# First-layer memory keys and values made inside the experts' loop in native fp32, and the down product put ahead of the up product from the seventh pair on

## What is computed

```python
# experts: the 256 tokens go to 4 of 32 experts each
u = xb @ w1[e] + b1[e]                      # w1[e]: 1024 x 2048 fp32, 8 MB
a = glu * sigmoid(SWIGLU_ALPHA * glu) * (lin + 1.0)
y = a @ w2[e] + b2[e]                       # w2[e]: 1024 x 1024 fp32, 4 MB

# first layer of the second model
h = x @ a_w_in                              # u, v, q_mem
mix = gmlp_mixer(u, v, ...)
kv = mem @ w_mem_kv[0]                      # mem: 256 x 1024, w_mem_kv[0]: 1024 x 512
k, v = split(kv)                            # keys and values of the memory, 4 heads of 64
s = softmax(q_mem . k * 64 ** -0.5); mem_out = s . v
x = layer_norm(ALPHA * x + concat(mix, mem_out) @ w_mix_out, ...)
```

## Time and profile before

| | |
|---|---|
| median of 3 runs | 1880.47 us |
| profiled execution, its own time | 1880.95 us |
| span of its instructions | 1879.2 us |
| PE busy | 1799.8 us (96%) |
| DVE, ACT busy | 773.2 us, 571.8 us |
| mean granted TensorE clock | 0.996 of full |
| DMA from slice 8 to slice 26 of 40 | 9 tenths or more, 426 to 432 GB/s in nearly all |
| chain that ended last | PE 79%, DMA 15%, DVE 3%, ACT 2% |

### The profile page before, as it was taken

The page is one execution under the profiler, slowest core; times in us unless marked ns, Lnnn a source line. Parts: engine busy times, 40 slices in busy tenths (PEclk is TensorE's granted clock), DMA queues, the critical chain, the costliest instruction groups (busy, mean ns, idle before and its releaser), DMA issues.

```text
span 1879.2 us, 24262 instructions
## 1 busy us (share of the span) xinstructions
PE 1799.8 (96%) x9774; PEld 1137.3 (61%) x9774; DVE 773.2 (41%) x1146; ACT 571.8 (30%) x913; POOL 16.5 (1%) x33
## 2 busy tenths in 40 slices
PE   7999999999999999989999999999999999999998
PEld 4799888733333333333333333337988888978886
DVE  3767655512112112121121111216676656676665
ACT  4444554410001100011000110005655545545552
POOL 0000001000000000000000000000000000000000
PEclk9999999999999999999999999999999999999999
DMA  9976755899999999999999999999356556336542
GB/s 353 328 249 226 246 198 189 316 427 426 431 431 430 431 430 430 429 431 429 430 431 429 432 430 430 431 430 341 134 180 199 182 202 202 121 105 205 197 170 100
DMA packets 155690, 592.39 MB, mean 315 GB/s; under 512 B 6735, under 2 KB 85775, under 8 KB 129120
## 3 DMA queue, kind: packets, MB, share of 16 engines
q1 hardware_dynamic: 153104, 582.90, 78.8%
q0 software_dynamic: 2512, 8.45, 1.4%
HBM read 590.26 MB, written 1.07 MB: 315 GB/s over the span
## 4 chain that ended last, share of the span: by engine, by line
PE 79%; DMA 15%; DVE 3%; ACT 2%; issue 1%; SPq 0%; DVEq 0%; ACTq 0%
PE psum L1781 18%; DMA expert_ring<-in_w_mlp_dram 13%; PE psum L426 9%; PE psum L1799 8%; PE psum L392 7%; PE psum L394 7%; PE psum L393 7%; PE psum L425 4%; PE psum L1765 4%; PE psum L410 2%; PE psum L1819 2%; PE psum L411 2%; PE psum L412 2%; DMA mixer_ring<-in_w_in_dram 1%; ACT expert_arena L1524 1%
## 5 line engine op out<-in xcount | busy, mean ns | idle before, releaser
L1781 PE MATMUL psum<-shared,expert_arena 128*64 128x512 f32 x1536 | 341.9, 597 | 18.9 <-DMA shared<-in_w_mlp_dram 18.9
L1627 DVE TENSOR_SCALAR expert_arena<-psum 128x512 f32<-128x512 f32 x32 | 22.1, 691 | 579.9 <-PE psum L1781 579.9
L1781 PEld LDWEIGHTS psum<-shared,expert_arena 128*64 128x64 f32 x1536 | 106.0, 137 | 238.6 <-issue 202.2
L426 PE MATMUL psum<-layer_x_parts,layer_w_hi 128*128 128x512 f32 x704 | 240.5, 396 | 0.4 <-DVE layer_x_parts L2131 0.4
L1530 ACT ACTIVATE expert_arena<-expert_arena 128x512 f32<-128x512 f32 x32 | 20.1, 629 | 559.4 <-DVE expert_arena L1627 559.4
L425 PE MATMUL psum<-layer_x_parts,layer_w_lo 128*128 128x256 f32 x616 | 171.8, 279 | 0.0
L353 DVE TENSOR_TENSOR mixer_w_lo<-mixer_ring,mixer_w_hi 128x1024 fp32r<-128x1024 f32 x96 | 116.3, 1222 | 88.7 <-ACT mixer_w_hi L348 88.1
L353 DVE TENSOR_TENSOR layer_w_lo<-slots_ahead,layer_w_hi 128x1024 fp32r<-128x1024 f32 x96 | 116.8, 1223 | 85.1 <-ACT layer_w_hi L348 85.1
L348 ACT CAST mixer_w_hi<-mixer_ring 128x1024 fp32r<-128x1024 f32 x96 | 100.0, 1048 | 151.6 <-PE psum L394 80.4
L426 PEld LDWEIGHTS psum<-layer_x_parts,layer_w_hi 128*128 128x128 f32 x704 | 125.8, 188 | 24.6 <-DVE layer_x_parts L2131 0.8
L392 PE MATMUL psum<-layer_w_hi,layer_x_parts 128*128 128x512 f32 (+1 forms) x368 | 134.2, 365 | 1.0 <-DVE layer_x_parts L2131 1.0
(11 more groups left out here) (324 smaller groups left out, 2630.2 us busy)
## 6 DMA issues: line engine op xcount, KB each, us to landing
shared<-in_w_mlp_dram SPq DMA_DIRECT2D x98, 2048.0 KB, 22.0
expert_ring<-in_w_mlp_dram SPq DMA_DIRECT2D x64, 2048.0 KB, 25.0
mixer_ring<-in_w_in_dram SPq DMA_DIRECT2D x38, 1024.0 KB, 7.0
slots_ahead<-in_w_mlp_dram SPq DMA_DIRECT2D x15, 2048.0 KB, 25.7
mixer_ring<-in_w_ada_dram SPq DMA_DIRECT2D x22, 1024.0 KB, 6.2
slots_ahead<-in_w_ffn_in_dram SPq DMA_DIRECT2D x22, 1024.0 KB, 5.0
memory_kv<-in_w_mlp_dram SPq DMA_DIRECT2D x15, 1024.0 KB, 24.7
kept<-in_w_mlp_dram SPq DMA_DIRECT2D x15, 1024.0 KB, 26.7
```

The lines of the kernel that those rows point to most:

```text
L426: last = self.nc.tensor.matmul(out, hi, both[:, k].rearrange("p h s -> p (h s)"), start=k == 0, stop=k == KC - 1)
L1781: last = nc.tensor.matmul(U[CAP * h:CAP * h + CAP, N * n:N * n + N], xg[:, k, j, :], expert_slot(M, k // 2)[:, at:at + N], start=False, st ...
```

## The change

1. In `on_sync`, `mem_2` and the final gain are issued ahead of the loop (after the last load for expert 1). The weights of the keys and values, `w_mem_kv_2[0]` (2 MB), are issued in the middle, behind the up pieces of expert 16, into `ahead`. The down pieces of expert 17 wait until the values are made (`memory_full`), since the memory's working tiles lie where they go.
2. PE runs `memory()` between pairs 7 and 8: 16 transposes in 4 groups through two banks that ACT empties, 16 products of 256 columns for the keys and 16 for the values, plain fp32. ACT copies the results out; PE waits for the last copy. After the loop ACT moves the values to `kv`.
3. From pair 6 on (TURN = 6) PE's order is `later_pairs_of`, with `down` ahead of `up`; ACT and DVE have loops to match (`turned`).
4. Layer 0 loses the jobs km0 and vm0 and their four units. Its scores now stand ahead of un1. The norm of v hangs on wsT0 instead of km0.

```diff
@@ experts @@
+    MIDDLE, TURN = PAIRS // 2, PAIRS // 2 - 2
...
@@ on_sync @@
                 second_odd(1, 1)
+                sp.dma_start(free(M["base"], 0, T, D), A["mem_2"][0].rearrange("(t p) d -> p t d", p=P)).then_inc(M["mem_here"], 16)
+                sp.dma_start(final_gain(M).unsqueeze(1), A["g_final"].rearrange("(o d) -> o d", o=1).partition_broadcast(P)).then_inc(M["fin_here"], 16)
...
+                    loads_of(1, MIDDLE)
+                    e = 2 * MIDDLE
+                    for k in range(UP):
+                        up_load_freed(e, e, k, True)
+                    sp.wait_ge(down_used, (e - 1) * DOWN + 1)
+                    sp.dma_start(M["ahead"][:, :], A["w_mem_kv_2"][0].rearrange("(p k) n -> p (k n)", k=KC)).then_inc(M["mem_here"], 16)
+                    for k in range(DOWN):
+                        down_load(e, e, k, 0, True)
+                    for k in range(UP):
+                        up_load_freed(e + 1, e + 1, k, True)
+                    sp.wait_ge(memory_full, VALUES)
+                    for k in range(DOWN):
+                        down_load(e + 1, e + 1, k, 1, True)
+                    loads_of(MIDDLE + 1, PAIRS - 1)
...
@@ on_scalar @@
+            def memory_rows_out():
+                for n in range(4):
+                    act.wait_ge(memory_full, n + 1)
+                    nc.scalar.copy(memT[:, 2 * n:2 * n + 2, :], bank[BG if n % 2 else BY].rearrange("p (k s) -> p k s", k=2)).then_inc(memory_out, 1)
+                act.wait_ge(memory_full, KEYS)
+                nc.scalar.copy(memory_keys(M), bank[BY].rearrange("p (a s) -> p a s", a=2)).then_inc(memory_out, 1)
+                act.wait_ge(memory_full, VALUES)
+                nc.scalar.copy(values_aside[:, :], bank[BG]).then_inc(memory_out, 1)
...
@@ on_vector @@
+                def turned(p):
+                    e = p * 2 + 1
+                    i = i0 + e
+                    gatedT_out(i - 1, 0)
+                    gate(r, e)
+                    dve.wait_ge(gathered, (r * PAIRS + p + 1) * 2)
+                    choose(r, p + 1)
+                    dve.wait_ge(down_used, (i - 1) * DOWN + 1)
+                    choose_own(e + 1, 0)
+                    y_out(i - 1)
+                    activate(i)
...
@@ on_tensor @@
+                    if ahead is not None and k == KC // 2:
+                        gather(ahead, 0)
...
+            def later_pairs_of(r, begin, end):
+                with pe.Fori(begin, end) as p:
+                    i = r * E + p * 2 + 1
+                    emptied(i - 1)
+                    down(i - 1, 0, r * PAIRS + p)
+                    up(i, r * PAIRS + p, 1, r * PAIRS + p + 1)
+                    scatter(i - 1, 0)
+                    gather(r * PAIRS + p + 1, 1)
+                    transposes(i)
+                    emptied(i)
+                    down(i, 1, r * (PAIRS - 1) + p)
+                    up(i + 1, r * PAIRS + p + 1, 0)
+                    scatter(i, 1)
+                    transposes(i + 1)
+
+            def memory():
+                pe.wait_ge(M["mem_here"], 16)
+                pe.wait_ge(down_used, 2 * MIDDLE * DOWN)
+                pe.wait_ge(xg_ready, 2 * MIDDLE + 2)
+                for n in range(4):
+                    if n >= 2:
+                        pe.wait_ge(memory_out, n - 1)
...
+                pe.wait_ge(M["mem_here"], 32)
+                pe.wait_ge(memory_out, 4)
+                for a in range(2):
+                    for k in range(KC):
+                        last = nc.tensor.matmul(bank[BY][:, N_MEM * a:N_MEM * a + N_MEM], w_mem[:, k, P * a:P * a + P], memT[:, k, :], start=k == 0, stop=k == KC - 1)
+                last.then_inc(memory_full, 1)
+                for t in range(T):
+                    for k in range(KC):
+                        last = nc.tensor.matmul(bank[BG][:, W_MEM * t:W_MEM * t + W_MEM], memT[:, k, P * t:P * t + P], w_mem[:, k, W_MEM:2 * W_MEM], start=k == 0, stop=k == KC - 1)
+                last.then_inc(memory_full, 1)
+                pe.wait_ge(memory_out, VALUES)
...
-            pairs_of(0, 0, middle)
+            pairs_of(0, 0, TURN)
+            later_pairs_of(0, TURN, MIDDLE)
+            memory()
...
@@ layer, i == 0 @@
         jobs.pair("vn1", "act", jobs.rows(w_in, W_MIX + N, W_MIX - N))
-        jobs.add("km0", "act", jobs.wide(w_kv[0], 0))
         for n in range(3):
             jobs.add(f"wsT{n}", "dve")
         jobs.add("bsT", "dve")
         jobs.pair("un0", "act", jobs.rows(w_in, 0))
         jobs.add("qm", "act", jobs.wide(w_in, 2 * W_MIX))
-        jobs.pair("un1", "act", jobs.rows(w_in, N, W_MIX - N))
         scores(0)
         scores(1)
+        jobs.pair("un1", "act", jobs.rows(w_in, N, W_MIX - N))
         for n in range(3):
             jobs.add(f"sv{n}", "dve")
-        jobs.pair("vm0", "act", jobs.rows(w_kv[0], W_MEM, W_MEM))
         weights_over(0)
```

More of the change, by code:

```diff
@@ L490, in __init__, with memory_keys @@
         self.ends = ends
+def memory_keys(M):
+    return free(M["shared"], RING_END, 2, N_MEM)
 def final_gain(M):
@@ L1267 @@
 AHEAD = 3
+RING_END = 3 * WIDE_SLOT
 LEAST = -3.0e38
@@ L1306, in experts @@
     own = ctx.enter_context(nc.sbuf_tensor("expert_own", [P, 2, P], F32R))
+    values_aside = ctx.enter_context(nc.sbuf_tensor("memory_values", [P, T * W_MEM], FP32))
+    mem_nat, memT = free(M["base"], 0, T, D), free(M["kept"], 0, KC, N_MEM)
+    w_mem = free(M["ahead"], 0, KC, 2 * W_MEM)
     b1, b2 = bias[:, 0:D], bias[:, D:D + N]
@@ L1557, in on_scalar @@
             further_rounds(act, one_round, flag[0])
+            act.wait_ge(memory_out, VALUES)
+            act.wait_ge(down_used, (E - 1) * DOWN)
+            nc.scalar.copy(free(M["kv"], 512, T * W_MEM), values_aside[:, :])
             nc.scalar.activation(warm, rstd, ACT.Sqrt)
@@ L1677, in one_round @@
                     y_out(i)
+                with dve.Fori(TURN, PAIRS - 1) as p:
+                    turned(p)
                 i = i0 + E - 1
@@ L1766, in gather, with up @@
                 last.then_inc(gathered, 1)
-            def up(i, pairs, j):
+            def up(i, pairs, j, ahead=None):
                 pe.wait_ge(bias_ready, 1)
```

66 lines of the change are left out of this document (48 added, 18 removed).

## The result

| | before | after |
|---|---|---|
| median of 5 runs each, us | 1880.47 | 1890.64 |
| lowest and highest | 1880.01, 1882.19 | 1889.83, 1892.47 |
| profiled execution: own time, span | 1880.95, 1879.2 | 1889.83, 1887.9 |
| loop's end, first "keep busy" product behind it | 1280.77 | 1296.12 |
| from there to the first write of x_res behind layer 0's mixer part | 90.17 | 83.50 |

The changed kernel takes 1.0053 of the time (95% interval 1.0042 to 1.0064): 10.2 us slower, where 2.1 us less were forecast. The last three lines of the table are read from the two profiled executions, and they add up to the difference of the spans: the loop is 15.35 us longer, layer 0 is 6.67 us shorter, the rest is the same. 15.35 - 6.67 = 8.7.

The account below looks back on a forecast made before the run. The weights' DMA was taken to bound the loop from pair 4, PE layer 0. Loop +3.4 and layer 0 -5.5 gave -2.1 on the profiled 1880.95, so 1878.9, or 1878.4 us as median; range 1873.8 to 1885.5.

Parts of the forecast that it names:

- `mem_2` and the gain: Ahead of the loop: both loads (1.57 MB, 3.7 us) fit a DMA hole of about 4.5 us; cost 0, bounds 0 and 1.
- `w_mem_kv`: Loop, DMA: the new piece costs 4.87 us in full; the last weights had 4.2 us of slack that can be spent.
- A later pair takes 56.0 us: Loop, PE in the new order: 54.55 - 0.90 + 1.32 + 1.0 = 56.0 us a pair, under the DMA's 58.5.
- `memory()`, 18.0 us: Middle of the loop, PE: transposes 3.3, key and value products 13.9, wait for ACT's last copy 0.8; bounds 16 and 21.
- Behind it the branch remains: Behind `memory()`, PE: 4.84 us of idle time as before, and 1.6 us lost behind it.
- The stop of the DMA, 2.3 us: Before up 18's first piece: 43.4 us of PE work plus some 2 of issue against 43.9 of cover; bounds 0 and 6.
- The end is the DMA's: Loop's tail: last weights at 1280.3, plus 3.5 for the last half product, 1283.8 against 1280.77; loop +3.4 us.
- Layer 0, -5.5: Layer 0: km0 gone -5.76, vm0 gone -1.4, one clock fall +1.7; -5.5 us, bounds -7.2 and -3.8.
- Rival (b): Loop behind the middle: PE becomes the bound, its lag not made up; 1889 with a clock fall each pair; chance 0.2.
- Rival (a): Loop and layer 0: DMA never stops, no clock falls; loop +0.9, layer -7.2, 1874.2 us; chance 0.2.

Follow-up runs that it names:

- the kernel with the arm moved: The changed kernel plus 16 matmuls at the end of TensorE's never-entered arm, shifting where the taken arm begins in its instruction block: 1884.25 us, ratio 1.0015.

## Why the prediction was wrong, point by point

- **`mem_2` and the gain, 0**: right. Without the branch TensorE waits for the same piece at 678.04, in the kernel before at 678.07.
- **`w_mem_kv`, +4.87 in full, less 4.2 of slack in the tail**: right. Without the branch the loop ends 0.83 us later; the text had +0.9 for a loop with no stop.
- **A later pair takes 56.0 us**: right, 56.1 to 56.2. TensorE waits 8.8 us for `emptied` in 13 waits and 6.5 in 7 for the activations between 880 and 1260, 0.68 and 0.93 each.
- **`memory()`, 18.0 us with the wait for the last copy**: right. 17.3, and the copy is out at 851.56, 17.9 after the start.
- **"Behind it the branch remains, 4.84 us of idle time", and 1.6 of clock**: this is the step that failed. It measured 12.63 us, and 2.3 of clock. The gap was read as a fixed price of the branch and carried over. It is the part of a fetch that queued products do not cover, times the number of fetches. From ACT's last copy at 851.56 to 863.55 it is 12.0 us, and the slow down product lost 9.40 - 7.09 = 2.3. Both counts moved: `memory()` ends in a wait, so nothing is queued any more (one fetch then shows in full, 6.5 to 6.8 us after the copy, where the kernel before showed 4.84), and the new code put the taken arm at the end of a block, which made it two. The second is worth 5.5 us of gap and 6.4 us of time, by the kernel with the arm moved.
- **The stop of the DMA, 2.3 us**: followed from that step. The count had 43.4 us of TensorE's work against 43.9 of cover and 2 us of issue. With 12.0 + 2.3 in place of 4.84 + 1.6 it is 7.9 longer, and the same count gives 10.2; 11.9 were seen, and the 1.7 between them stay open. The bounds, 0 and 6, were too narrow since they did not take in the price of the branch, which was given none.
- **The end is the DMA's, so each us of stop is one of loop**: right: 11.9 of stop, and 14.5 us between the loop ends with and without the branch. 0.7 of the rest is there before the branch already (678.74 against 678.04), some 1.9 I can't place.
- **Layer 0, -5.5**: -6.7. Every wait was right to 0.1 us. The fall of the clock was not there (1.00 in every stretch from 1290 to 1380), and without it the text had -7.2; 0.5 is left.
- **Rival (b)** gave 1889 with TensorE behind in every later pair. The time was near, the mechanism was not: period and waits are the forecast's. **Rival (a)** gave 1874.2 for a DMA that never stops and no fall of the clock in layer 0; the kernels with no branch and with the branch at pair 3, which have no stop, measured 1877.5 and 1878.2, with profiled executions of 1875.87 and 1875.89, near the low end of their own runs. Why their medians lie 2 us above these isn't settled.

The idea of using TensorE's slack held: without the branch the change is 3.6 us faster than the kernel before. With the branch kept and a gap of 4.8 us it would at best have been about level, an estimate from the kernel with the arm moved: 3.1 us over its kernel before, less 2.3 us of gap, less some 0.9 of clock (2.5 us lost in the down product behind its gap, against 1.6 in the kernel before).

## What to carry to other kernels

An idle time that a profile calls "issue" behind a branch is no constant. Ask what was queued ahead of it (here a wait right before the branch left nothing queued, and 1.9 us more of the fetch showed), where its target lies in its block, and whether the place can pay for one fetch or for two. After a run, the packets of q8 and the records between them say which it was. When code moves around a branch, price it from one fetch to two in the range; and put the branch where the bound engine is another one and several pairs with slack follow, as at pair 3 here.

Where one engine runs full and the other has slack, the slack is a budget of lateness in one stretch: everything inserted in that stretch is to be summed, and the excess goes one to one into the end.

## What the runs showed of the hardware that was not expected

- Counted from TensorE's last wait ahead of the branch to its next product, one fetch of instructions beside a full DMA takes 6.5 to 7.5 us, whether products are queued or not: in the kernel before 836.71 to 843.53 (6.8; 2.0 of it queued products, the rest the gap), with the old order 7.47 less the 0.6 of ACT's copy (6.8), with the arm moved 7.17 less 0.6 (6.5), with the branch at pair 3 547.39 to 554.88 (7.5), with the new order alone 834.35 to 841.16 (6.8). Two take 12.0 (the change) and 12.5 (720.72 to 733.23, two pairs earlier). At the loop's end, where the DMA is full too, one takes 6.1 (1282.15 to 1288.24). So a gap at a branch is this time less what was queued.
- Matmuls in an arm that never runs changed the time by 6.4 us (0.3%). No-operations written there changed neither the gap (12.78 against 12.63 us) nor, clear of the 6 records between two executions, the distance of the packets.
- A wait of 2.4 us in layer 0 left the granted clock at 1.00, where 2.12 in the mixer was followed by 0.50. Behind the long gap it fell to 0.50, and the first down product took 9.40 us.
- An fp32 product takes four instructions of a block: the count with four gives shifts of 104, 88 and 64 where the traces have 116, 96 and 52.
- What stays open: whether the place of an arm in its block can be known beforehand to within a few instructions. My count of two to a product told one fetch from two in the eight kernels whose arm was not moved by many matmuls, and failed for the two that were; but also there its places differ from the traces' by up to 40 records.
